# Scores and values of two attention heads issued by turns on two halves of the TensorE array

## The chip, the core and the metric

The kernel runs on one core of a Trainium2 chip. Its time is the device time of one execution in microseconds (us), taken as the median of three runs: 1239.64 us (1238.21 to 1241.14). The engines are TensorE (PE; its weight loads are shown as PEld), VectorE (DVE), ScalarE (ACT), GpSimd (POOL) and SyncE (SP, which here only issues transfers).

## The reference, cut to what matters

Two transformer blocks run one after the other on 256 tokens of width 1024. The first block has a pooling mixer beside an attention of 8 heads of 64 (att 1), then a feed-forward layer that picks 16 experts for each token and head. The second block has 8 heads with a forget gate and 8 heads with a banded mask and a relative bias (att 2, heads 0 to 7 and 8 to 15), then a convolutional feed-forward layer. Shortened, the attention parts are:

```python
# block 1, 256 positions are one block of keys: plain causal attention
s_own = jnp.einsum('bhcd,bhld->bhcl', q_c, k_own) * HEAD_DIM ** -0.5
p = jax.nn.softmax(jnp.where(k_pos <= q_pos, s_own, NEG), axis=-1)
o = jnp.einsum('bhcl,bhld->bhcd', p_own, v_own)

# block 2, heads 0 to 7: the logits also get a difference of running sums of log f
logits = jnp.einsum('bhqd,bhkd->bhqk', qb, k) * scale
logits = logits + cb[..., :, None] - cum[..., None, :]
# block 2, heads 8 to 15
logits = jnp.einsum('bhcqd,bhckd->bhcqk', qc, k_band) * (d ** -0.5) + bias
```

## The kernel before, in words

Every engine runs one program written out by hand, and waits on counters that the others raise. There is no planner for the stretches that change; the order in the code is the order on each queue. A name such as `("masked", att, i, tt)` is an event; `pe.wait_ge(made, ...)` waits for VectorE, `acted` for ScalarE, `done` for TensorE.

**Layout.** Queries and keys lie with two heads on the 128 partitions: the even head on partitions 0 to 63, the odd one on 64 to 127. A head's scores (`head_scores`, line 1460) are two fp32 products with 64 rows: 128 queries by 128 keys, and 128 queries by 256 keys, into one accumulator bank. Heads 0 to 7 of att 2 add to each a product with 8 rows that spreads the running sum of log f (`cum`). An fp32 product is two passes over the array, each with a load of its weights, so four records for a head of att 1 and eight for one with the forget gate. VectorE adds the mask and takes the row minimum (`masked`, line 925; the queries are scaled by -1/8, so it is the maximum of the logits), ScalarE takes exponentials (`exps`, 510), VectorE normalizes (`normed`, 909 and 912), TensorE transposes three 128x128 pieces (`turn`, 1468), ScalarE copies them out (`turned`, 517), and TensorE multiplies by the values (`values`, 1479 and 1480), with an output of 64 partitions: the even head's in the lower half of a bank, the odd head's in the upper half. VectorE or ScalarE reads that bank when both are there (`attended`, 938; `y_high`, 801; `attended_low`, 942).

**Order.** Both attentions are loops over steps i. On TensorE step i holds the scores of head i, then a large group of work that has nothing to do with this head (48 passes of projections with f32r weights, line 1408 or 1430, or branch products, 1559), then the transpose of head i-2, then the values of head i-3, then small products of the pooling mixer (1580, 1581, 1589). The same steps stand on VectorE: the mask of head i, `normed` of head i-1, splits of weights into a high and a low part (867), and in att 1 chunks of a matrix-vector product for the modulation (`ada`, 878). ScalarE has in step i the exponentials of head i, the copy of the step's projection (`copy_unit`, 504), roundings of weights (`split_high`, 500), and the transpose's copy. The steps of att 1 take 86 to 169 us of the profiled execution, those of att 2 922 to 1026 us.

**Banks.** There are eight accumulator banks. `Banks.take` gives the one freed first and lets TensorE wait for the event that frees it; `give` puts it back at the end of the queue, with that event, when the work is issued. So the order of all takes and gives decides which event each group of matmuls waits for:

```python
def take(self, pe, name):
    b, events = self.free.pop(0)
    self.where[name] = b
    for event in events:
        pe.wait_ge(*event)
```

A bank of scores is freed by the mask of its head, one of a projection by its copy, one of a transpose by `turned`.

Of the kernel before, what the change touches and what calls it, by code (L numbers as in the profile page):

```python
# [15 lines left out]
P = 128  # L16
T = 256
# [182 lines left out]
def build(nc, x_in, c_in, consts, bands_in, bmask_in, cols, relb, rows, w_ada, w_in, w_pool, w_br, w_out, w_q, keysT, uv, w_in2, w_f2,  # L200
          w_out2, w_up, w_down, out):
    with ExitStack() as ctx:
# [25 lines left out]
        probT = sb("probT", [P, 4, 384])  # L228
# [9 lines left out]
        ps = [ctx.enter_context(nc.psum_tensor(f"ps{i}", [P, 512], F32)) for i in range(8)]  # L238
# [12 lines left out]
        ident, ones = K("ident"), K("ones")  # L251
        ALL, tile = slice(0, T), [slice(0, P), slice(P, T)]
# [75 lines left out]
        cum, ncum = stat[0:8, 0:256], stat[0:8, 256:512]  # L328
# [13 lines left out]
        done = Mark(sem("s_pe"))  # L342
        acted = Mark(sem("s_act"))
        made = Mark(sem("s_dve"))
        marks = [*loaded, *half_loaded.values(), *once.values(), *arrived_in.values(), stored, high, low, done, acted, made]
        where = {}
# [41 lines left out]
        heads = {1: 8, 2: 16}  # L388
        cols_of = [slice(0, P), slice(P, 3 * P)]
# [993 lines left out]
        def tensor(e):  # L1383
            pe = Engine(e)
            banks = Banks(where)

            def group(name):
                return ps[banks.take(pe, name)]
# [59 lines left out]
                    ins.then_inc(*done.put(("rope", name, j0)))  # L1448
                    banks.give(("rope", name, j0), made, ("sin", name, j0))

            def head_scores(att, i):
                q3, k3, _, _, h = head_of(att, i)
                r, j = 64 * (h % 2), h // 2
                o = group(("heads", att, i))
                for tt in range(2):
                    terms = [(q3[r:r + 64, j, tile[tt]], k3[r:r + 64, j, 0:P + P * tt])]
                    if att == 2 and i < 8:
                        terms.append((ident[0:8, h:h + 1].broadcast_to([8, P]), cum[:, 0:P + P * tt]))
                    for m, (l, s) in enumerate(terms):
                        ins = e.matmul(o[:, cols_of[tt]], l, s, start=(m == 0), stop=(m == len(terms) - 1))  # L1460
                ins.then_inc(*done.put(("heads", att, i)))
                banks.give(("heads", att, i), made, ("masked", att, i, 1))

            def turn(att, i):
                o = group(("turn", att, i))
# [3 lines left out]
                ins.then_inc(*done.put(("turn", att, i)))  # L1469
                banks.give(("turn", att, i), acted, ("turned", att, i))  # L1470

            def values(att, i):
                _, _, v3, _, h = head_of(att, i)
                if i % 2 == 0:
                    group(("out", att, i // 2))
                r, pt = 64 * (i % 2), probT[:, i % 4, :]
                o = ps[where["out", att, i // 2]][r:r + 64, 0:T]
                pe.wait_ge(acted, ("turned", att, i))
                e.matmul(o, v3[:, 0, h * 64:(h + 1) * 64], pt[:, 0:T], start=True, stop=False)
                e.matmul(o[:, P:T], v3[:, 1, h * 64:(h + 1) * 64], pt[:, T:384], start=False, stop=True).then_inc(  # L1480
                    *done.put(("pv", att, i)))
                if i % 2:
                    banks.give(("out", att, i // 2), made, ("y", att, i // 2))

            def turned_rows(tt):

# [36 lines left out]
            for k0 in (0, 4):  # L1523
                pe.wait_ge(loaded[SLOT_OF["in", 0]] if k0 else half_loaded["in", 0], ("in", 0))
                for tt in range(2):
                    for k in range(k0, k0 + 4):
                        pe.wait_ge(acted, ("modulated", k))
                        ins = e.matmul(mixer[tt][:, :], h_sb[:, k, tile[tt]], w[:, k, :], start=(k == 0), stop=(k == KD - 1))
# [34 lines left out]
                    banks.give(("quarter", q), made, ("gated", 4 * br + z))  # L1563

            for i in range(11):
                if i < 8:
                    head_scores(1, i)
                if i < 7:
                    columns(*beside1[i], xs, lambda k: [], acted)
                if i >= 7:  # L1570
                    branch(0, i - 7)
                if 2 <= i <= 9:
                    turn(1, i - 2)
                if i >= 3:
                    values(1, i - 3)
                if i < 4:
                    o = group(("window", i))
                    pe.wait_ge(once["bands"], 0)
                    pe.wait_ge(acted, ("u", 1))
                    e.matmul(o[:, 0:T], ut[:, 0, i * P:(i + 1) * P], bands[:, i, 0:T], start=True, stop=False)  # L1580
                    e.matmul(o[:, P:T], ut[:, 1, i * P:(i + 1) * P], bands[:, i, T:T + P], start=False, stop=True).then_inc(
                        *done.put(("window", i)))
                    banks.give(("window", i), acted, ("window", i))
                if 1 <= i < 5:
                    g = i - 1
                    o = group(("mix", g))
                    pe.wait_ge(once["wp"], 0)
                    pe.wait_ge(acted, ("window", g))
                    e.matmul(o[:, 0:T], wp[:, g * P:(g + 1) * P], pT[:, g, :], start=True, stop=True).then_inc(
                        *done.put(("mix", g)))  # L1590
                    banks.give(("mix", g), acted, ("mix", g))

            for half in range(2):
                o = group(("gate1", half))
                pe.wait_ge(made, "mod2")
                for k in range(4):
                    c = 16 + 4 * half + k
                    ins = e.matmul(o[:, k * P:(k + 1) * P], mod[:, c:c + 1].broadcast_to([P, P]), ident, start=True,
                                   stop=True)
# [135 lines left out]
            for n in range(256):  # L1735
                tt, k = divmod(n, 128)
# [6 lines left out]
                for half in range(2):  # L1743
                    ins = e.matmul(acc[half][:, :], diag[:, n % 8, :],  # L1744
                                   row_buf[n][:, D + half * 512:D + (half + 1) * 512], start=(k == 0), stop=(k == 127))
# [27 lines left out]
            o = group("forget")  # L1773
            pe.wait_ge(made, "wf low")
            for k in range(KD):
                for n, (w, r) in enumerate(((wf_hi, hi_r), (wf_hi, lo_r), (wf_lo, hi_r))):
                    ins = e.matmul(o[0:8, 0:T], w[:, k, :], r[:, k, :], start=(k == 0 and n == 0),
                                   stop=(k == KD - 1 and n == 2))
# [31 lines left out]
            o = group("own sums")  # L1810
            pe.wait_ge(made, "ncum")
            for tt in range(2):
                ins = e.transpose(o[:, 8 * tt:8 * tt + 8], ncum[:, tile[tt]], ident[0:8, 0:8])
# [3 lines left out]
            for i in range(19):  # L1817
                if i == 8:
                    pe.wait_ge(acted, unit("in2", 4, 0))
                    pe.wait_ge(made, unit("in2", 4, 2))  # L1820
                    pe.wait_ge(acted, unit("in2", 3, 2))
                if i == 3:
                    pe.wait_ge(made, ("v", 2, 1))
                if i == 11:
                    pe.wait_ge(made, ("v", 5, 1))
                if i < 16:
                    head_scores(2, i)
                if i < 6:
                    kind, c, z = beside2[i]
                    if c == 5:  # L1830
                        tokens(kind, c, z, xs, both)
                    else:
                        columns(kind, c, z, xs, both, made if (c, z) == (4, 2) else acted)
                if 11 <= i < 15:
                    out2(0, (i - 11) // 2, (i - 11) % 2, range(4))
                if i == 17:
                    for half in range(2):
                        for tt in range(2):
                            out2(1, half, tt, range(2))
                if 2 <= i <= 17:  # L1840
                    turn(2, i - 2)
                if i >= 3:
                    values(2, i - 3)
            for tt in range(2):
                for half in range(2):
                    out2(1, half, tt, range(2, 4))
# [182 lines left out]
```

## Time and profile before

| | |
|---|---|
| median of three runs | 1239.64 us |
| the profiled execution | 1240.34 us, its span 1238.4 us |
| TensorE busy | 1092.4 us (88%) |
| VectorE busy | 821.9 us (66%) |
| ScalarE busy | 428.2 us (35%) |
| GpSimd busy | 292.4 us (24%) |
| mean granted TensorE clock | 0.955 of full speed |
| scores (line 1460), records | 96 with 64 rows, 32 with 8 rows |
| values (1479, 1480), records | 48 and 48 |

The span is the time from the first to the last instruction of the profiled execution. Matmuls are pipelined: a record's duration runs on into the next, so what a group costs is the distance of its start to the start of the next group. The expert rows are fetched between about 230 and 890 us.

### The profile page before, as it was taken

To read this page: it belongs to the slowest core of one execution; us is meant where nothing else is said; L and a number is where in the kernel's file an instruction comes from. 1 tells how busy PE (TensorE), PEld (TensorE's weight loads), DVE (VectorE), ACT (ScalarE), POOL (GpSimd) and SP (SyncE) were. 2 spreads that over 40 slices of the span, in tenths; PEclk is the share of its full clock that TensorE was granted. 3 is DMA by queue.
4 is the path that set the end of the run, shared out by engine and by line. 5 is a ranking of instruction groups with operands and counts; after the bars stand their busy time and mean duration, and the time that the engine had idled before them with its cause. 6 is when DMAs were issued, how large, how long until landed. Compare 5 with 4: busy or idle time off the path is not lost.

```text
span 1238.4 us, 13445 instructions
## 1 busy us (share of the span) xinstructions
PE 1092.4 (88%) x4938; PEld 723.5 (58%) x4938; DVE 821.9 (66%) x1891; ACT 428.2 (35%) x896; POOL 292.4 (24%) x260
## 2 busy tenths in 40 slices
PE   5999899899999987887788787788899999999997
PEld 3798785654445542333233333333698668999986
DVE  6696753767777677788877555545645545888753
ACT  3534441322322232122222111111554443666541
POOL 0000000345354442543544444443000000000000
PEclk8999899899999997988998999989999988999999
DMA  9977834799999999999999999999753311545530
GB/s 380 428 306 301 308 128 180 287 402 415 421 421 421 421 422 420 421 422 420 422 421 420 421 422 421 423 420 411 319 221 121 118 68 69 205 176 197 201 140 35
DMA packets 47878, 389.39 MB, mean 314 GB/s; under 512 B 5442, under 2 KB 5826, under 8 KB 7236
## 3 DMA queue, kind: packets, MB, share of 16 engines
q0 software_dynamic: 36864, 268.45, 52.3%
q1 hardware_dynamic: 10948, 120.07, 25.0%
q8 instruction: 40, 0.66, 0.2%
q14 instruction: 26, 0.21, 0.0%
HBM read 387.45 MB, written 1.05 MB: 314 GB/s over the span
## 4 chain that ended last, share of the span: by engine, by line
PE 52%; DMA 29%; DVE 12%; ACT 4%; issue 1%; POOL 1%; SPq 0%; DVEq 0%; POOLq 0%
DMA ring<-in_uv,idx 25%; PE ps L1408 16%; PE ps L1744 16%; PE ps L1869 5%; DMA ring<-in_w_ada 4%; DVE ring L1224 3%; PE ps L1614 2%; PE ps L1800 2%; PE ps L1559 2%; PE ps L1460 2%; PE ps L1430 2%; DVE ring_r L867 2%; DVE ring L878 2%; PE ps L1630 1%; POOL ring L484 1%
## 5 line engine op out<-in xcount | busy, mean ns | idle before, releaser
L1744 PE MATMUL ps<-ring,probT 128*128 128x512 f32 x1024 | 497.1, 631 | 106.9 <-ACT probT L732 106.8
L484 POOL DMA_INDIRECT ring<-in_uv,idx x256 | 292.2, 1141 | 563.5 <-PE ps L1744 307.0
L1224 DVE CUSTOM_DVE_ANT_0 ring<-h2t,ring 128x1024 f32<-128x1024 f32 x256 | 310.1, 1222 | 173.2 <-DMA ring<-in_uv,idx 172.8
L1744 PEld LDWEIGHTS ps<-ring,probT 128*128 128x128 f32 x1024 | 200.0, 201 | 354.0 <-issue 202.8
L1408 PE MATMUL ps<-util_r,ring_r 128*128 128x256 f32 x1312 | 216.6, 282 | 2.3 <-DVE ring_r L867 2.2
L867 DVE TENSOR_TENSOR ring_r<-ring,ring_r 128x1024 fp32r<-128x1024 f32 x134 | 158.3, 1220 | 54.7 <-ACT ring_r L500 54.7
L1408 PEld LDWEIGHTS ps<-util_r,ring_r 128*128 128x128 f32 x1312 | 181.0, 188 | 7.0 <-issue 3.9
L500 ACT ACTIVATE ring_r<-ring 128x1024 fp32r<-128x1024 f32 x134 | 134.6, 1049 | 46.5 <-DMA ring<-in_w_in 23.4
L727 ACT ACTIVATE prob<-prob 128x2 f32<-128x2 f32 (+2 forms) x94 | 19.2, 204 | 372.2 <-DVE prob L1224 372.1
L1408 PE MATMUL ps<-h_r,ring_r 128*128 128x256 f32 x704 | 125.2, 281 | 0.6 <-DVE util_r L1196 0.6
L732 ACT ACTIVATE probT<-ct,prob 128x128 f32<-128x128 f32 x256 | 85.1, 392 | 73.7 <-DVE prob L1230 73.5
L1408 PEld LDWEIGHTS ps<-h_r,ring_r 128*128 128x128 f32 x704 | 108.0, 188 | 0.8 <-issue 0.8
L878 DVE CUSTOM_DVE_ANT_0 ring<-h2t,ring 128x1024 f32<-128x1024 f32 x44 | 51.2, 1219 | 9.6 <-DMA ring<-in_w_ada 9.4
L1869 PE MATMUL ps<-ring_r,util_r 128*128 128x512 f32 x176 | 50.1, 395 | 0.0
L510 ACT ACTIVATE prob<-prob,mx 128x128 f32<-128x128 f32 (+1 forms) x48 | 21.5, 448 | 56.2 <-DVE mx L925 56.1
L1630 PEld LDWEIGHTS ps<-h_sb,ring 128*128 128x128 f32 x128 | 24.5, 192 | 24.8 <-issue 24.0
L1869 PEld LDWEIGHTS ps<-ring_r,util_r 128*128 128x128 f32 x176 | 32.9, 187 | 8.0
L1630 PE MATMUL ps<-h_sb,ring 128*128 128x256 f32 x128 | 36.0, 381 | 0.0
L1430 PE MATMUL ps<-ring_r,util_r 128*128 128x256 f32 x288 | 34.9, 281 | 0.0
L1430 PEld LDWEIGHTS ps<-ring_r,util_r 128*128 128x128 f32 x288 | 34.1, 188 | 0.7 <-issue 0.7
L1559 PE MATMUL ps<-area_r,ring_r 128*128 128x256 f32 x192 | 26.4, 301 | 6.1 <-DVE area_r L890 4.7
L1230 DVE TENSOR_TENSOR prob<-prob 128x2 f32<-128x2 f32 (+2 forms) x94 | 14.6, 155 | 23.2 <-ACT prob L727 23.2
(209 smaller groups left out, 1019.6 us busy)
## 6 DMA issues: line engine op xcount, KB each, us to landing
ring<-in_w_in SPq DMA_DIRECT2D x13, 2048.0 KB, 12.4
ring<-in_w_up SPq DMA_DIRECT2D x11, 2048.0 KB, 7.7
ring<-in_w_ada SPq DMA_DIRECT2D x7, 2048.0 KB, 7.7
ring<-in_w_down SPq DMA_DIRECT2D x6, 2048.0 KB, 7.7
ring<-in_w_ada SPq DMA_DIRECT2D x8, 1024.0 KB, 15.0
ring<-in_w_out SPq DMA_DIRECT2D x4, 2048.0 KB, 7.7
ring<-in_w_q SPq DMA_DIRECT2D x3, 2048.0 KB, 10.7
ring<-in_w_br SPq DMA_DIRECT2D x2, 2048.0 KB, 10.4
```

The lines of the kernel that those rows point to most:

```text
L484: e.indirect_dma_start(out=row_buf[n], out_offset=None, in_=uv, in_offset=bass.IndirectOffsetOnAxis(ap=idx[:, tt, k:k + 1], axis=0)).then_inc(
L500: e.activation(hi, w, ACT.Copy).then_inc(*high.put(q))
L732: e.activation(diag[:, n % 8, :], ident, ACT.Copy, scale=wt[:, tt, n % 128:n % 128 + 1]).then_inc(*acted.put(("diag", n)))
L867: e.tensor_tensor(lo, w, hi.bitcast(F32), ALU.subtract).then_inc(*low.put(q))
L878: e.tensor_tensor_reduce(wv, crow, wv, 1.0, 0.0, ALU.mult, ALU.add, mod[:, 4 * c + j:4 * c + j + 1]).then_inc(*made.put(("ada", c, j)))
L1224: e.tensor_tensor_reduce(u, h2t[:, tt, :], u, 1.0, 0.0, ALU.mult, ALU.add, av[:, tt, n % 128:n % 128 + 1]).then_inc(*made.put(("dot", n)))
L1408: ins = e.matmul(o[:, jj * T:(jj + 1) * T], w[:, k, :], r[:, k, :], start=(k == 0 and n == 0), stop=(k == KD - 1 and n == 2))
L1430: ins = e.matmul(o, r[:, k, tt * P:(tt + 1) * P], w[:, k, :, :], start=(k == 0 and n == 0), stop=(k == KD - 1 and n == 2))
L1559: ins = e.matmul(o[:, jj * T:(jj + 1) * T], w[:, k, jj * P:(jj + 1) * P], x3[:, k, :], start=(jj == 0 and k == 0 and n == 0), stop=(jj == ...
L1630: ins = e.matmul(bank(("q", h))[:, jj * T:(jj + 1) * T], w[:, k, z * P:(z + 1) * P], h_sb[:, k, :], start=(k == 0), stop=(k == KD - 1))
L1744: ins = e.matmul(acc[half][:, :], diag[:, n % 8, :], row_buf[n][:, D + half * 512:D + (half + 1) * 512], start=(k == 0), stop=(k == 127))
L1869: ins = e.matmul(ps[where["down", tt, half]][:, :], h[:, k, tile[tt]], w[:, 0, HALF[half]], start=(k == 0 and n == 0), stop=(k == KF - 1 a ...
```

## The change

`head_scores` becomes `pair_scores`. It is called in every even step and issues the scores of heads i and i+1: for each of the two query tiles first the even head's product on partitions 0 to 63, then the odd head's on 64 to 127, each into its own bank. With the forget gate the four products with 8 rows follow behind all four with 64 rows. Both banks are taken at the start of the step. `values` becomes `pair_values`, called in every even step from 4 on for heads i-4 and i-3, so that the even head's values come one step later than before, and the odd head's in the same step; the two write to the two halves of the output's partitions by turns. It waits for the later of the two transposed probabilities. In both loops the order of the rest stays. Two waits for the projected values move from steps 3 and 11 to 4 and 12.

```diff
-            def head_scores(att, i):
+            def pair_scores(att, i):
                 q3, k3, _, _, h = head_of(att, i)
-                r, j = 64 * (h % 2), h // 2
-                o = group(("heads", att, i))
+                j, summed = h // 2, att == 2 and i < 8
+                o = [group(("heads", att, i + a)) for a in range(2)]
                 for tt in range(2):
-                    terms = [(q3[r:r + 64, j, tile[tt]], k3[r:r + 64, j, 0:P + P * tt])]
-                    if att == 2 and i < 8:
-                        terms.append((ident[0:8, h:h + 1].broadcast_to([8, P]), cum[:, 0:P + P * tt]))
-                    for m, (l, s) in enumerate(terms):
-                        ins = e.matmul(o[:, cols_of[tt]], l, s, start=(m == 0), stop=(m == len(terms) - 1))
-                ins.then_inc(*done.put(("heads", att, i)))
-                banks.give(("heads", att, i), made, ("masked", att, i, 1))
+                    for a in range(2):
+                        r = slice(64 * a, 64 * a + 64)
+                        ins = e.matmul(o[a][:, cols_of[tt]], q3[r, j, tile[tt]], k3[r, j, 0:P + P * tt], start=(tt == 0),
+                                       stop=(tt == 1 and not summed))
+                        if tt == 1 and not summed:
+                            ins.then_inc(*done.put(("heads", att, i + a)))
+                if summed:
+                    for a in range(2):
+                        for tt in range(2):
+                            ins = e.matmul(o[a][:, cols_of[tt]], ident[0:8, h + a:h + a + 1].broadcast_to([8, P]),
+                                           cum[:, 0:P + P * tt], start=False, stop=(tt == 1))
+                        ins.then_inc(*done.put(("heads", att, i + a)))
+                for a in range(2):
+                    banks.give(("heads", att, i + a), made, ("masked", att, i + a, 1))
...
-            def values(att, i):
+            def pair_values(att, i):
                 _, _, v3, _, h = head_of(att, i)
-                if i % 2 == 0:
-                    group(("out", att, i // 2))
...
+                o = group(("out", att, i // 2))
+                pe.wait_ge(acted, ("turned", att, i + 1))
+                for s in range(2):
+                    for a in range(2):
+                        pt, v = probT[:, (i + a) % 4, :], v3[:, s, (h + a) * 64:(h + a + 1) * 64]
+                        ins = e.matmul(o[64 * a:64 * a + 64, P * s:T], v, pt[:, T * s:T * s + (P if s else T)],
+                                       start=(s == 0), stop=(s == 1))
+                        if s == 1:
+                            ins.then_inc(*done.put(("pv", att, i + a)))
+                banks.give(("out", att, i // 2), made, ("y", att, i // 2))
...
-                if i < 8:
-                    head_scores(1, i)
+                if i < 8 and i % 2 == 0:
+                    pair_scores(1, i)
...
-                if i >= 3:
-                    values(1, i - 3)
+                if i >= 4 and i % 2 == 0:
+                    pair_values(1, i - 4)
...
-                if i < 16:
-                    head_scores(2, i)
+                if i < 16 and i % 2 == 0:
+                    pair_scores(2, i)
...
-                if i >= 3:
-                    values(2, i - 3)
+                if i >= 4 and i % 2 == 0:
+                    pair_values(2, i - 4)
```

## Rows read from the trace of the kernel before

**Rows 1.** The chain of waits over the whole span, shares by engine

```profile
PE 52%; DMA 29%; DVE 12%; ACT 4%; issue 1%; POOL 1%; SPq 0%; DVEq 0%; POOLq 0%
```

**Rows 2.** Stage table: stretch, its length, busy us of each engine, granted clock, transfers

```profile
101.60:143.10 41.50, 41.50 (x307) 36.72 (x306) 28.80 (x74) 19.19 (x51) 0.00 (x0) 1.00 0.74 280
...
922.00:957.50 35.50, 35.50 (x246) 30.02 (x245) 17.74 (x36) 19.75 (x44) 0.00 (x0) 1.00 0.39 138
```

**Rows 3.** TensorE timeline, first attention: start, us, line, tiles, count, [idle before, releaser]

```profile
101.64 0.92 PE L1460 MATMUL ps<-area 64*128 64x128 f32 x4
102.48 5.95 PE L1408 MATMUL ps<-util_r,ring_r 128*128 128x256 f32 x48
...
109.78 0.92 PE L1460 MATMUL ps<-area 64*128 64x128 f32 x4
...
148.68 5.46 PE L1559 MATMUL ps<-area_r,ring_r 128*128 128x256 f32 x24 [4.67 <-DVE area_r L890]
...
155.23 3.12 PE L1559 MATMUL ps<-area_r,ring_r 128*128 128x256 f32 x24
...
165.09 3.10 PE L1559 MATMUL ps<-area_r,ring_r 128*128 128x256 f32 x24 [1.47 <-DVE util L933]
...
168.92 2.05 PE L1598 MATMUL ps<-ct,mod 128*128 128x128 f32 x16
```

**Rows 4.** VectorE timeline, first attention: masks of heads 1 and 5, copy of values

```profile
106.57 0.29 DVE L925 CUSTOM_DVE_ANT_0 prob<-ps,ct 128x128 f32<-128x128 f32 x1
...
134.86 0.28 DVE L925 CUSTOM_DVE_ANT_0 prob<-ps,ct 128x128 f32<-128x128 f32 x1
...
143.19 0.42 DVE L938 COPY area<-ps 128x256 f32<-128x256 f32 x1 [0.38 <-PE ps L1480]
```

**Rows 5.** ScalarE timeline, first attention: copy of step 4's projection

```profile
126.12 0.57 ACT L504 ACTIVATE util<-ps 128x512 f32<-128x512 f32 x1
```

**Rows 6.** TensorE timeline, second attention

```profile
922.15 0.48 PE L1460 MATMUL ps<-area 64*128 64x128 f32 x2
...
924.23 5.94 PE L1408 MATMUL ps<-util_r,ring_r 128*128 128x256 f32 x48
930.10 0.48 PE L1460 MATMUL ps<-area 64*128 64x128 f32 x2
...
954.60 0.65 PE L1479 MATMUL ps<-probT,area 128*64 128x256 f32 x2
...
955.40 0.48 PE L1460 MATMUL ps<-area 64*128 64x128 f32 x2
...
973.45 0.49 PE L1460 MATMUL ps<-area 64*128 64x128 f32 x2
...
1023.76 0.49 PE L1468 MATMUL ps<-ct,prob 128*128 128x128 f32 x3
```

**Rows 7.** The chain in order of time: start, us, engine, tile, line, count

```profile
250.27 0.86 PE ps L1630 x4
...
893.76 17.04 PE ps L1408 x144
```

**Rows 8.** Stage table around three idle stretches of TensorE, columns as in rows 2

```profile
148.70:153.90 5.20, 5.20 (x24) 5.20 (x25) 4.56 (x14) 0.99 (x4) 0.00 (x0) 0.50 0.91 315
...
842.40:846.10 3.70, 0.00 (x1) 0.01 (x1) 1.68 (x5) 0.66 (x3) 0.94 (x1) 1.00 1.01 421
847.00:850.30 3.30, 3.30 (x5) 1.35 (x4) 1.90 (x4) 0.00 (x0) 0.99 (x1) 0.50 1.03 427
...
987.00:997.00 10.00, 9.14 (x24) 5.75 (x23) 6.92 (x25) 6.81 (x18) 0.00 (x0) 0.50 0.01 2
```

**Rows 9.** VectorE timeline, second attention: masks of heads 2, 7 and 8

```profile
940.23 0.29 DVE L925 CUSTOM_DVE_ANT_0 prob<-ps,small 128x128 f32<-128x128 f32 x1 [2.80 <-PE ps L1460]
...
979.52 0.28 DVE L925 CUSTOM_DVE_ANT_0 prob<-ps,small 128x128 f32<-128x128 f32 x1
...
982.96 0.28 DVE L925 CUSTOM_DVE_ANT_0 prob<-ps,util 128x128 f32<-128x128 f32 x1
```

More of the change, by code:

```diff
@@ L1470, in turn @@
                 banks.give(("turn", att, i), acted, ("turned", att, i))
-            def values(att, i):
+            def pair_values(att, i):
                 _, _, v3, _, h = head_of(att, i)
-                if i % 2 == 0:
-                    group(("out", att, i // 2))
[L1476 to L1483, printed above, removed]
+                o = group(("out", att, i // 2))
[8 more added lines that the diff above has]
+                banks.give(("out", att, i // 2), made, ("y", att, i // 2))
             def turned_rows(tt):
@@ L1821, in tensor @@
                     pe.wait_ge(acted, unit("in2", 3, 2))
-                if i == 3:
+                if i == 4:
                     pe.wait_ge(made, ("v", 2, 1))
-                if i == 11:
+                if i == 12:
                     pe.wait_ge(made, ("v", 5, 1))
-                if i < 16:
-                    head_scores(2, i)
+                if i < 16 and i % 2 == 0:
+                    pair_scores(2, i)
                 if i < 6:
```

## The prediction, made before the changed kernel was run

> **What bounds the kernel now.** I read the chain of waits first: TensorE holds 52% of it, row fetches and weight loads 29%, VectorE 12% [rows 1]. The fetches are the expert-row loop between about 230 and 890 us, which the change does not touch. It touches two stretches, read in the stage table [rows 2]: the first attention (TensorE busy 41.5 of 41.5 us up to 143) and the second (35.5 of 35.5 us up to 957; behind 975 two other engines set the pace, [rows 9]). What is full there could gain from less TensorE work; but an engine that works without gaps in a fixed order also stops at the first wait that moves ahead of it. So the next views are the timelines of TensorE [rows 3, 6], VectorE [rows 4] and ScalarE [rows 5].
>
> **Price of a head now.** A 256-column fp32 pass takes 0.215 us (four in 0.86 us [rows 7]), a 128-column pass half, 0.11. A head's scores are two of each, 0.65 us, yet 0.84 us lie between their start and the next group's, 101.64 to 102.48 [rows 3]: 0.19 us more. The 48 passes between two heads' scores take 5.87 us, 924.23 to 930.10 [rows 6], against 5.68 for 48 in an undisturbed run (144 in 17.04 us [rows 7]): another 0.19 us. An entry and an exit thus cost 0.4 us together, 0.2 per change of form. It fits the forget-gate heads: 2.08 us (922.15 to 924.23 [rows 6]) for 1.30 us of passes, which is four changes (64 rows, 8 rows, 64, 8, 128). A head's values: 0.80 us (954.60 to 955.40 [rows 6]) for 0.65 us, so 0.15 for that change.
>
> **What the change removes.** Per pair of heads it removes an entry and an exit of the 64-row form and one entry of the half-column form: 0.55 us. With the forget gate, 12 changes become 4, so 8 go: 7 x 0.2 + 0.15 = 1.55 us. Four pairs of each of three kinds: 4 x 0.55 + 4 x 1.55 + 4 x 0.55 = 10.6 us of TensorE time. The passes themselves are as many as before.
>
> **Overlap of the two halves.** Nothing in the trace has two heads alternating, so I bound it. Full overlap makes a pair as long as one head: -0.65 us per pair of scores or values. The other end: each change of half costs like a change of form, three a pair, +0.6 us. Each pass needs its own weights first, and the second head follows the first only after both passes of its fp32 product, so most of a half's time cannot be shared: only the last pass of one and the first of the other could run together. I take -0.1 us per pair of scores and -0.2 per pair of values.
> The Trainium skill (TensorEngine Tiling (Array Packing), Key Properties) says that a change of tiling mode drains the array, which agrees with the 0.2 us above, and that tiles work independently of each other, for which no row here speaks. By that rule the overlap is nearer its full end, and the time is that of rival A.
>
> **The price in the first attention: banks.** Accumulator banks are handed out in a ring of eight, first freed first taken, and TensorE waits in program order. I wrote out the ring. Before, the group of 48 passes of step 2 (102.48) takes the bank of head 0. Now two heads take banks in step 0, so it takes that of head 1, which is free when VectorE has masked head 1. VectorE does that at 106.57 and ends about 107.2 [rows 4]; it comes after work on ada weights that TensorE does not influence. The ring written out this way names the gating product as what the last branch group waits for at 165.09, and the trace shows that wait, 1.47 us [rows 3].
> So TensorE, with step 2's pair done at about 103.1, stands until 107.3: 4.2 us. Its queue holds everything else of the stage. From there: 7.2 us to step 3's group (102.48 to 109.78 [rows 3], less the drain of the entry, 0.1), 114.5; its 5.8 us, transpose, window and mix, 1.6, to 121.9; pair (4,5), 1.5, 123.4; 48 passes end 129.2. ScalarE's copy of them was at 126.12 [rows 5], now 129.4, 3.3 later. Behind that copy in ScalarE's queue are two weight roundings, VectorE's two splits follow them, then its copy of values and an ada chunk, then the mask of head 5 at 134.86 [rows 4], now 138.2 to 138.8. Pair (6,7) takes the bank of head 5, so TensorE waits for that, 0.6 us. Then 1.5 + 5.8 + 0.4 + 1.5 us: the values of head 3 are ready at 148.1, where VectorE takes them at 143.19 [rows 4], with only 0.38 us of its own slack. Everything up to the branch group at 148.68 follows on that: **+4.9 us**.
> Given back behind it: from 148.68 to 168.92 [rows 3] are 20.24 us. Now: branch groups 5.26, 2.95, 2.95, 3.05; three transposes 1.26; two pairs of values 3.2; 18.7 in all. The 1.47 us wait is hidden, because the last branch group now takes another bank and the gated one falls to the values behind it: **-1.6 us**. What is late next there is nothing: the following matmuls run on without a gap to 200.
>
> **Clock.** Behind the 4.67 us stall before 148.68 the granted clock was 0.50 of full speed (the 1.2 GHz level) for 5.2 us, and 24 passes took 5.46 us where 24 take 3.12 at full clock [rows 3, 8]: 2.3 us. Behind 3.7 us of idleness up to 846.10 it was 0.50 too [rows 8]. The new stall of 4.2 us lies between those two, so I count a second such loss, **+2.3 us**; it passes through the same chain whole. Bounds: 0, and 5 us if it lasted as long as the 10 us from 987 to 997 [rows 8].
>
> **Second attention.** First five steps: three forget-gate pairs (0-1, 2-3, 4-5) and values 0-1, with heads 6 and 7 not begun. Before, 922.15 to 973.45 [rows 6] is 51.3 us. Now: 2.97 + 5.73 + 5.62 + 0.1, then 2.97 + 5.73 + 0.33 + 5.62 + 0.43, then 2.97 + 5.76 + 0.42 + 1.43 + 5.71 + 0.43 = 46.2 us: -5.1 us. No mask is late here: VectorE stands idle until TensorE's scores come (2.80 us before head 2 [rows 9]), so the banks are free in time. From 975 to 991 VectorE and ScalarE drive each other: mask, exponentials, rounding, split, next mask, 3.44 us a head (979.52 to 982.96 [rows 9]). The work of TensorE does not stand in that ring, so the 5 us stay and nothing is added. From 989 on TensorE is the bound again. Pairs (12,13) and (14,15) with their values take off 1.1. But VectorE masks head 15 only after its part of y from values 10 and 11, which come a step late, so the transposes of heads 13 to 15 wait for it: 1.6 to 2.3 us, and the values of head 12 fall behind that, 0.6: +2.9 in the upper case, which I take. The end (values 15, y, last products) keeps its distance to the last transpose at 1023.76 [rows 6]: values 14 now wait there too, 0.6 us, beside a rounding of ScalarE. Of the clock: from 987 to 997 it was 0.50 [rows 8], and TensorE lost some 3.2 us on the path from 989 on. At full clock the sum is -5.0 - 1.1 + 2.9 - 3.2 = **-6.4 us**. The stretch stays as loosely filled, so I expect the clock low again for 4 to 7 us of work on the path, half of which is lost: **+2.7**.
>
> **Sum.** +4.9 - 1.6 + 2.3 - 6.4 + 2.7 = +1.9 us. Overlap on the path (8 pairs of scores by 0.1, 7 of values by 0.2; others lie under stalls): -2.2. In all -0.3 us on the profiled execution's 1240.34 (span 1238.4 and 1.9 around it), which is 0.7 above the median 1239.64. A median is what will be compared, so I go from it: 1239.64 - 0.3 = 1239.34, told as **1239.3 us**: no change.
>
> **Rivals.**
> *A, the halves do overlap and the clock holds.* -0.2 per pair of scores and -0.4 of values make -4.4 instead of -2.2; without the low clock after 987, 2.7 less. 1.9 - 4.4 - 2.7 = -5.2: 1234.4 us; with the overlap alone -2.5, 1237.1. For it: separate rows, banks and columns. Against: the clock fell in that same loose stretch before [rows 8]. Chance 0.27.
> *B, slower: changing halves is a change of form.* If a pass on rows 64 to 127 drains what runs on rows 0 to 63, three changes a pair at 0.2 us return on each of the 8 score pairs on the path, +4.8, with no overlap: 1.9 + 4.8 = +6.7, 1246.3 us; if half of it is hidden, +4.3, 1243.9. Decisive from 0.1 us a change on. For it: the heads of [rows 6] pay 0.2 us for every change. Against: those are changes of size, and these are not. Together with a longer stall at 103 (a longer low clock, +0.8) chance 0.22.
> *C, no stall at 103.* If head 1's bank were not needed, only gains are left: -1.6 - 6.4 + 2.7 - 2.2 and 0.55 us from each of the two pairs before 143 = -8.6: 1231.0 us. Against it the wait at 165.09, which the ring names. Chance 0.06.
> The forecast keeps 0.45.
>
> **Range.** 1233.5 to 1244.5: A whole, the near half of B, not C. What this kernel's timings can tell from no change is about 0.2%, 2.5 us. Faster by more: A, C and a part of the forecast, 0.34. Slower: B and the forecast with no overlap and the longer low clock, 0.25. Within: 0.41.
>
> **What would show it.** In the timeline of TensorE after: a stall of about 4 us after the second pair of scores, ended by VectorE's mask (wrong, if TensorE goes on at 103); a granted clock of 0.50 behind it; the stall at 165.09 gone; the branch group of 148.68 near 153 to 156; the first pair of scores of the second attention at about 3.0 us where two heads took 4.2; the last transpose minus the first score 95 instead of 101.6 us. A pair of scores without the forget gate shows the overlap: 1.5 us from its start to the next group's is none, 1.3 and less is overlap, 2.1 is rival B. The forecast is wrong if the two stretches do not move in opposite directions by about 5 us each.

## The result and the profile after

The changed kernel takes 1231.84 us, the median of five runs (1230.42 to 1232.97); the kernel before, beside it, 1239.48. The ratio is 0.993, with a 95% interval of 0.9917 to 0.9943: 7.6 us faster, where no change was forecast and the range ended at 1233.5. The profiled execution took 1231.68 us, its span is 1229.8 (before 1238.4). TensorE was busy for 1080.7 us (88%), VectorE 821.5, ScalarE 428.9, GpSimd 289.9, and the mean granted clock was 0.937 of full speed (0.942 to 0.950 in the other four runs), lower than the 0.955 of before.

The shares of the chain of waits are those of [rows 1] within a point, so this view does not tell where the time went:

```profile
PE 52%; DMA 29%; DVE 13%; ACT 3%; issue 1%; POOL 1%; SPq 0%; DVEq 0%; POOLq 0%
```

The timeline of TensorE in the first attention answers to [rows 3] (start, us, engine, line, tiles, count, [idle before, releaser]; 1459 are now the scores, 1488 the values, 1476 the transposes, 1568 the branches, 1607 the groups that were 1598):

```profile
101.63 0.93 PE L1459 MATMUL ps<-area 64*128 64x128 f32 x8
107.26 8.58 PE L1408 MATMUL ps<-util_r,ring_r 128*128 128x256 f32 x48 [4.70 <-DVE mx L925]
...
124.28 0.93 PE L1459 MATMUL ps<-area 64*128 64x128 f32 x8
125.14 5.95 PE L1408 MATMUL ps<-util_r,ring_r 128*128 128x256 f32 x48
...
131.35 0.87 PE L1488 MATMUL ps<-probT,area 128*64 128x256 f32 x8
132.15 0.70 PE L1598 MATMUL ps<-area,h2t 128*128 128x256 f32 x2
...
140.58 0.93 PE L1459 MATMUL ps<-area 64*128 64x128 f32 x8 [1.73 <-DVE mx L925]
...
154.06 4.64 PE L1568 MATMUL ps<-area_r,ring_r 128*128 128x256 f32 x24 [5.56 <-DVE area_r L890]
...
166.11 3.08 PE L1568 MATMUL ps<-area_r,ring_r 128*128 128x256 f32 x24
169.12 0.87 PE L1488 MATMUL ps<-probT,area 128*64 128x256 f32 x8
169.92 2.05 PE L1607 MATMUL ps<-ct,mod 128*128 128x128 f32 x16
```

Three things are to be seen. The stall after the second pair of scores is there, ended by VectorE's mask as the ring of banks had it, and a second one before the last pair. The wait of 1.47 us before the last branch group is gone. And a group of eight score records takes 0.86 us to the next group's start (124.28 to 125.14), the same as four did in [rows 3] (0.84 us); eight of the values take 0.80 us (131.35 to 132.15), as four did in [rows 6]. A pair costs as much as one head.

The second attention, same view, answers to [rows 6]:

```profile
924.60 0.93 PE L1459 MATMUL ps<-area 64*128 64x128 f32 x8
925.46 1.57 PE L1466 MATMUL ps<-stat,ct 8*128 8x128 f32 x8
926.96 11.62 PE L1408 MATMUL ps<-util_r,ring_r 128*128 128x256 f32 x96
...
975.56 0.55 PE L1476 MATMUL ps<-ct,prob 128*128 128x128 f32 x3 [1.66 <-DVE prob L912]
976.89 1.55 PE L1488 MATMUL ps<-probT,area 128*64 128x256 f32 x8 [0.78 <-ACT probT L517]
979.82 1.65 PE L1459 MATMUL ps<-area 64*128 64x128 f32 x8
...
1006.68 0.52 PE L1476 MATMUL ps<-ct,prob 128*128 128x128 f32 x3 [1.80 <-DVE prob L912]
...
1017.38 0.49 PE L1476 MATMUL ps<-ct,prob 128*128 128x128 f32 x3
```

The first two heads with the forget gate end after 2.36 us (924.60 to 926.96), where one took 2.08. From the first score to the last transpose are 92.8 us; it was 101.6.

The stage table of after (stretch, length, busy us of TensorE, its weight loads, VectorE, ScalarE and GpSimd, granted clock, transfers) shows first the two stretches of [rows 2], then those in which the clock was low, and one that was low before:

```profile
101.60:143.10 41.50, 35.07 (x265) 32.73 (x265) 25.25 (x65) 16.53 (x44) 0.00 (x0) 0.88 0.65 242
922.00:957.50 35.50, 35.50 (x287) 32.87 (x286) 20.21 (x46) 21.57 (x49) 0.00 (x0) 1.00 0.43 154
...
107.30:113.20 5.90, 5.90 (x28) 5.90 (x29) 1.73 (x9) 2.56 (x10) 0.00 (x0) 0.50 0.96 347
150.80:157.60 6.80, 3.54 (x17) 3.57 (x17) 6.80 (x15) 0.16 (x1) 0.00 (x0) 0.50 0.90 340
976.80:990.30 13.50, 11.15 (x41) 7.26 (x42) 9.97 (x34) 8.87 (x26) 0.00 (x0) 0.50 0.09 37
1007.60:1014.20 6.60, 6.19 (x19) 4.65 (x20) 4.47 (x7) 2.92 (x5) 0.00 (x0) 0.50 0.37 156
1020.00:1036.00 16.00, 13.16 (x86) 11.22 (x85) 9.36 (x23) 6.17 (x12) 0.00 (x0) 1.00 0.36 132
```

Of the kernel before, the same view at the same place of the program as the last row:

```profile
1034.80:1041.40 6.60, 6.54 (x30) 6.02 (x28) 1.11 (x1) 1.72 (x3) 0.00 (x0) 0.50 0.63 271
```

The time by stages, before and after, from starts in the two timelines:

| start of | before | after | difference, and step |
|---|---|---|---|
| first branch group | 148.68 | 154.06 | +5.4 |
| line 1598 / 1607 | 168.92 | 169.92 | +1.0, so -4.4 |
| first score, second attention | 922.15 | 924.60 | +2.5, so +1.5 |
| its last transpose | 1023.76 | 1017.38 | -6.4, so -8.8 |
| first product behind the second attention (1408) | 1044.95 | 1036.31 | -8.6, so -2.3 |
| end of the span | 1238.4 | 1229.8 | -8.6, so 0 |

### The profile page after: what moved, and what is told of

It reads as the page before. It is cut to its first block, busy times and chain, and to the rows that moved or that the text cites. A ratio compares the mean times of both kernels' runs of the same rounds, so it can differ in the third digit from the quotient of the medians.

```text
span 1229.8 us, 13453 instructions
## 1 busy us (share of the span) xinstructions
PE 1080.7 (88%) x4938; PEld 717.4 (58%) x4938; DVE 821.5 (67%) x1891; ACT 428.9 (35%) x896; POOL 289.9 (24%) x260
## 4 chain that ended last, share of the span: by engine, by line
PE 52%; DMA 29%; DVE 13%; ACT 3%; issue 1%; POOL 1%; SPq 0%; DVEq 0%; POOLq 0%
DMA ring<-in_uv,idx 25%; PE ps L1753 16%; PE ps L1408 16%; PE ps L1878 5%; DMA ring<-in_w_ada 4%; DVE ring L1224 3%; DVE ring L878 2%; PE ps L1623 2%; PE ps L1809 2%; DVE ring_r L867 2%; PE ps L1568 2%; PE ps L1430 2%; PE ps L1639 2%; POOL ring L484 1%; ACT L727 1%
## 5 line engine op out<-in xcount | busy, mean ns | idle before, releaser
L1753 PE MATMUL ps<-ring,probT 128*128 128x512 f32 x1024 | 507.8, 643 | 97.5 <-ACT probT L732 97.4
L1753 PEld LDWEIGHTS ps<-ring,probT 128*128 128x128 f32 x1024 | 204.3, 205 | 349.6 <-issue 208.6
L1408 PE MATMUL ps<-util_r,ring_r 128*128 128x256 f32 x1312 | 219.6, 285 | 6.4 <-DVE mx L925 4.7
L1408 PEld LDWEIGHTS ps<-util_r,ring_r 128*128 128x128 f32 x1312 | 184.2, 192 | 9.7 <-DVE mx L925 5.4
```

Of the source, the lines that this page charges most:

```text
L1408: ins = e.matmul(o[:, jj * T:(jj + 1) * T], w[:, k, :], r[:, k, :], start=(k == 0 and n == 0), stop=(k == KD - 1 and n == 2))
L1753: ins = e.matmul(acc[half][:, :], diag[:, n % 8, :], row_buf[n][:, D + half * 512:D + (half + 1) * 512], start=(k == 0), stop=(k == 127))
```

## The experiments

All are timed against the kernel before, which gave 1239.66, 1240.59 and 1239.99 us in the three sets of runs. Line numbers move a little from kernel to kernel.

**By turns, or only next to each other?**

```diff
 # pair_scores; pair_values likewise with s
-                for tt in range(2):
-                    for a in range(2):
+                for a in range(2):
+                    for tt in range(2):
```

> The changed kernel, but within each pair the first head's products are all issued before the second head's, for scores and for values; steps, banks and waits are the same. Theory 1 (the halves of the array run at the same time only because products on the two halves stand next to each other in the queue, and this overlap of 0.64 us a pair is what the prediction sized too small): a pair goes back from 0.86 to about 1.5 us, with some 8 pairs of scores and 7 of values on the path +9 us, 1239 to 1241 us. Theory 2 (each half has its own queue of products, so it looks ahead over a whole head of four passes): a pair stays at 0.86 us and the time at 1232. Rival (the gain comes from fewer changes of form and from the clock, and the overlap lies under stalls): a pair at 1.5 us, but the time within 2 us of 1232.

Measured: 1231.91 us (1230.91 to 1232.08), ratio 0.9938 (0.9921 to 0.9954), the time of the changed kernel, as theory 2 has it. Three narrow windows of TensorE's timeline, each from just before the first score record, tell how close the records start. The changed kernel, up to 101.80:

```profile
101.63 0.38 PE L1459 MATMUL ps<-area 64*128 64x128 f32 x2
```

This kernel, up to 102.02:

```profile
101.99 0.39 PE L1459 MATMUL ps<-area 64*128 64x128 f32 x2
```

The kernel before, up to 101.80:

```profile
101.64 0.37 PE L1460 MATMUL ps<-area 64*128 64x128 f32 x1
```

Two records of 0.37 us each lie in 0.38 and 0.39 us: both halves start at once, although in this kernel all passes of the first head stand ahead of the second head's in the queue. That the second record is the other head's shows in the forms. Of this kernel's line 1459, the records from 101.98 to 102.25:

```profile
L1459 PE MATMUL ps<-area x4: 272/322/373, 102.0 to 102.2; 64*128 64x128 f32 x4
```

These are all four passes with 128 keys, two of each head, and none yet with 256 keys, though the first head's two of these stand ahead of the second head's in the queue. The turns of the change add nothing; heads on different halves that stand next to each other are enough. The Trainium skill (TensorE: Matmul & The Clock Gate, Part 3: Packing small matmuls) says that matmuls start and end strictly in the order of the program; here a second head's first pass starts beside the first head's first pass and thus before its second, so the trace does not bear that out, while the page's picture of packed tiles starting almost together fits.

**Is it the halves?** The odd head's queries and keys are taken from the partitions of the even one, so both heads use rows 0 to 63; the kernel leaves out the odd heads' scores. Everything else stays.

```diff
-                        r = slice(64 * a, 64 * a + 64)
+                        r = slice(0, 64)
```

> The changed kernel, but both heads of a pair take their scores from partitions 0 to 63, so the odd heads use the even head's queries and keys; instruction counts, banks, waits and changes of form are the same. Theory 1 (different row halves are what lets two products run at the same time, worth 0.64 us a pair): a pair of scores takes 1.50 us instead of 0.86, with 6 to 8 of 12 pairs on the path +4 to +5 us, 1236 to 1237 us. Rival (two products into different banks overlap in any case, or the pairs are hidden): 1232 us.

Measured: 1239.17 us (1236.64 to 1242.47), ratio 0.9994 (0.9982 to 1.0006). TensorE's timeline:

```profile
101.68 1.57 PE L1459 MATMUL ps<-area 64*128 64x128 f32 x8
107.31 0.58 PE L1408 MATMUL ps<-util_r,ring_r 128*128 128x256 f32 x1 [4.06 <-DVE mx L925]
...
927.16 1.57 PE L1459 MATMUL ps<-area 64*128 64x128 f32 x8
928.66 1.57 PE L1466 MATMUL ps<-stat,ct 8*128 8x128 f32 x8
930.16 13.14 PE L1408 MATMUL ps<-util_r,ring_r 128*128 128x256 f32 x96
```

The pair takes 1.50 us (927.16 to 928.66) instead of 0.86: 0.64 more, which is the whole of the second head. The first theory has the cause right, and its time is 2 us too low. Without the overlap of the scores the kernel is no faster than before, although it has all the savings in changes of form, and its values still overlap (0.80 us a pair). That its time is near the one I had forecast (1239.3) is chance. Of the 7.3 us between this kernel and the changed one, the overlap of the 8 pairs of scores that I had counted on the path explains 5.1. The rest goes with a cost that I had not expected: behind the first pair of the second attention 96 passes take 13.14 us for 11.62, and the 48 behind the third pair and behind the last pair of the first attention take 1.5 us more each, at the low clock. The run does not separate the two.

**What must stand next to what?** In the pairs with the forget gate each head's 8-row products go right behind its own 64-row ones: 64, 8, 64, 8 instead of 64, 64, 8, 8.

```diff
                 if summed:
                     for a in range(2):
+                        r = slice(64 * a, 64 * a + 64)
+                        for tt in range(2):
+                            e.matmul(o[a][:, cols_of[tt]], q3[r, j, tile[tt]], k3[r, j, 0:P + P * tt], start=(tt == 0), stop=False)
                         for tt in range(2):
                             ...
```

> The changed kernel, but in the pairs with the forget gate each head's two products with 8 rows stand right behind its own two with 64 rows, so that the two heads' 64-row products are no longer neighbours in the queue. Theory (what overlaps is only what stands next to each other and uses other rows): the pair goes from 2.36 us to 2.36 + 0.65 (overlap lost) + 0.4 (two more changes of form) = 3.4 us or more; three to four such pairs on the path make +3 to +4 us: about 1235.5 us. Rival (a head on the upper rows runs beside whatever is ahead of it, the 8-row products too): only the two changes are paid, 2.8 us a pair, +1.5 us: 1233.3 us.

Measured: 1239.71 us (1235.07 to 1241.25), ratio 0.9991 (0.998 to 1.0002). Line 1467 holds the products with 64 rows here, 1469 those with 8:

```profile
941.53 0.92 PE L1467 MATMUL ps<-area 64*128 64x128 f32 x4
942.38 0.92 PE L1469 MATMUL ps<-stat,ct 8*128 8x128 f32 x4
943.23 0.92 PE L1467 MATMUL ps<-area 64*128 64x128 f32 x4
944.07 0.92 PE L1469 MATMUL ps<-stat,ct 8*128 8x128 f32 x4
944.92 7.47 PE L1408 MATMUL ps<-util_r,ring_r 128*128 128x256 f32 x48
```

The pair takes 3.39 us (941.53 to 944.92) for 2.36, so 1.03 more, which is the overlap of 0.64 and two changes of form at 0.2: the first theory. Nothing on the upper rows runs beside the 8-row products ahead of it. But the total is 4 us above what that theory gave. Four such pairs cost 4.1; from first score to last transpose are 101.8 us (925.08 to 1026.92) for 92.8, so 4.9 us are left, and most of them stand behind the pairs, as the stage table shows for the second:

```profile
945.00:950.00 5.00, 5.00 (x30) 5.00 (x31) 4.96 (x11) 2.03 (x3) 0.00 (x0) 0.66 0.65 279
```

The clock, at 1.00 throughout this stretch of the changed kernel, is at 0.66 behind the pair of 3.4 us, and 48 passes take 7.3 us for 5.8. The same holds behind the first pair (96 passes, 12.9 us for 11.6) and the third (48, 7.3 for 5.7): 4.4 us in all. I had not expected that. That nothing else takes part was not tested.

**Scores alone, values alone.** `pair_scores` or `pair_values` is put back to the form of before, with its call:

```diff
 # scores only; the loop of the second attention likewise
-                if i >= 4 and i % 2 == 0:
-                    pair_values(1, i - 4)
+                if i >= 3:
+                    values(1, i - 3)
 # values only
-                if i < 8 and i % 2 == 0:
-                    pair_scores(1, i)
+                if i < 8:
+                    head_scores(1, i)
```

> Only the scores are paired; values head by head in their old steps. Theory 1: the stall at 103 us stays (two score banks are taken in one step), the second attention gains about 1.8 us for each of the four forget-gate pairs and 1 us for each later pair on the path: 1236 us. Rival (scores and values gain alike, or values more): 1238 or more.

> Only the values are paired; scores head by head in their old steps. Theory 1: no stall at 103 us, since the order in which banks are freed does not move until step 3; each pair of values on the path (two behind 148 us, four or five in the second attention) takes off 0.8 us, which makes 5 us: 1234.5 us. Rival (values lie under waits for ScalarE's copy): 1238 or more.

Measured: scores alone 1237.37 us (1236.07 to 1238.53), ratio 0.9978 (0.9968 to 0.9987); values alone 1234.13 (1231.99 to 1237.13), 0.9949 (0.9933 to 0.9966). The timelines of the first attention, scores alone (1567 are the branches):

```profile
107.47 7.84 PE L1408 MATMUL ps<-util_r,ring_r 128*128 128x256 f32 x48 [4.70 <-DVE mx L925]
...
154.49 5.33 PE L1567 MATMUL ps<-area_r,ring_r 128*128 128x256 f32 x24 [5.52 <-DVE area_r L890]
...
170.73 1.45 PE L1567 MATMUL ps<-area_r,ring_r 128*128 128x256 f32 x10 [1.47 <-DVE util L933]
```

and values alone (1560 are the branches, 1599 the groups that were 1598):

```profile
148.84 5.07 PE L1560 MATMUL ps<-area_r,ring_r 128*128 128x256 f32 x24 [6.01 <-DVE area_r L890]
...
161.33 3.08 PE L1560 MATMUL ps<-area_r,ring_r 128*128 128x256 f32 x24
165.14 2.05 PE L1599 MATMUL ps<-ct,mod 128*128 128x128 f32 x16
```

The stall at 103 belongs to the scores, and the end of the 1.47 us wait to the values (by the ring, to the later taking of their bank). Values alone bring line 1599 3.8 us forward (168.92 to 165.14); scores alone bring the second attention, first score to last transpose, from 101.6 to 91.9 us, values alone only to 99.6. The two parts gain in different attentions. Finer differences there tell nothing: the code of the changed kernel's second attention takes 90.4 to 92.8 us in the four profiles that have it.

**One attention at a time.** The unchanged attention keeps `head_scores` and `values`:

```diff
 # second only; first only has the same in the loop of the second
-                if i < 8 and i % 2 == 0:
-                    pair_scores(1, i)
+                if i < 8:
+                    head_scores(1, i)
```

> The second attention paired, the first as before. Theory 1 (the second attention gives 9 us, the first loses 1 and the row loop does not differ): 1239.7 - 9 to 11, 1229 to 1231 us, a little faster than the changed kernel. Rival (a part of the 9 us is the clock after 1034 us, which falls or not by chance): 1233.

> The first attention paired, the second as before. Theory 1: the two stalls and the second low clock cost 5.4 us up to the branch group, 4.4 come back behind it: 1239.7 + 1, between 1240 and 1242 us. Rival (the first attention gains on balance): 1238 or less.

Measured: second alone 1230.54 us (1227.92 to 1231.22), ratio 0.9916 (0.9897 to 0.9936); first alone 1240.81 (1237.84 to 1244.15), 1.0003 (0.999 to 1.0015). In the first attention all that the pairs save is eaten by the stall; the gain of the change is the second attention's.

**Does the bank make the stall?** In the first attention the odd head's bank goes back to the queue one step later, so that the next taker is given another; first for heads 1, 3, 5 and 7, then for 1, 3 and 5:

```diff
-                for a in range(2):
+                for a in range(2 if att == 2 or i == 6 else 1):
                     banks.give(("heads", att, i + a), made, ("masked", att, i + a, 1))
 # at the end of step i of the first attention
+                if i < 6 and i % 2:
+                    banks.give(("heads", 1, i), made, ("masked", 1, i, 1))
```

> The changed kernel, with one edit: in the first attention the bank of each odd head goes back into the ring at the end of the next step, so no group of that step takes it. Theory 1 (the stall of 4.7 us at 103 us, the one of 1.7 us at 139 us and the low clock behind the first one cost what the first stretch lost): both stalls gone, the branch group at 148.5 us instead of 154.1, the 1.5 us wait before the last branch group is back: 5 us less, 1227 us. Rival (VectorE's chain of splits, ada chunks and copies ends that stretch anyway and TensorE's delay was mostly hidden): less than 2 us, 1230 or more.

> The kernel with the late banks of the first attention, but only for heads 1, 3 and 5; head 7's bank goes back at once, as in the changed kernel. Written out, the ring then gives the last branch group the bank of an output (free early) and the waiting values the one of the gating product. Theory 1 (what the late banks won before 148 us was lost again in that wait and in the low clock behind it, 2.3 + 1.6 us): branch group at 148 us and no wait at 163, the following products start at about 165 us instead of 169; 1.5 to 4 us less than the 1229 us with all banks late: 1226 us. Rival (the wait for the gating product only moves to the values): 1229.

Measured: four heads 1229.01 us (1226.53 to 1230.83), ratio 0.991 (0.989 to 0.9931); three heads **1225.44** us (1224.54 to 1226.22), 0.9882 (0.9866 to 0.9899), which beats both kernels. Four heads stay 2 us above what the theory gave. With them the stalls at 103 and 139 go, but the ring moves a wait to the last branch group:

```profile
148.23 5.46 PE L1568 MATMUL ps<-area_r,ring_r 128*128 128x256 f32 x24 [7.27 <-DVE area_r L890]
...
163.76 4.62 PE L1568 MATMUL ps<-area_r,ring_r 128*128 128x256 f32 x24 [2.26 <-DVE util L933]
169.12 2.05 PE L1609 MATMUL ps<-ct,mod 128*128 128x128 f32 x16
```

With three it is gone as well:

```profile
101.72 0.93 PE L1459 MATMUL ps<-area 64*128 64x128 f32 x8
102.58 5.94 PE L1408 MATMUL ps<-util_r,ring_r 128*128 128x256 f32 x48
...
148.19 5.46 PE L1568 MATMUL ps<-area_r,ring_r 128*128 128x256 f32 x24 [8.79 <-DVE area_r L890]
...
165.28 2.05 PE L1609 MATMUL ps<-ct,mod 128*128 128x128 f32 x16
```

The branch group starts at 148.19, 0.5 us ahead of before, though TensorE now stands idle for 8.79 us before it: VectorE's product (line 890) sets that start, and up to there the saving of TensorE is worth nothing. Behind it the stage is shorter.

**Do the values of the second attention need pairing?** The version above, with `values` of before in the second attention:

```diff
-                if i >= 4 and i % 2 == 0:
-                    pair_values(2, i - 4)
+                if i >= 3:
+                    values(2, i - 3)
```

> The version with the later bank for heads 1, 3 and 5 (1225.4 us), but in the second attention the values run head by head as in the kernel before; scores stay paired. Theory: in the second attention it is the paired scores that bring the gain (scores alone left 92.1 us from first score to last transpose, values alone 99.8), because the odd head's earlier transposes and y then come a step sooner again; so about 1225 us, within 1.5 of the version it is derived from. Rival: paired values count by their overlap (0.6 us each) and by the change of form they save; five pairs lie on TensorE's path, so 3 to 4 us are lost: 1228.5 us.

Measured: 1226.67 us (1225.27 to 1226.97), ratio 0.9891 (0.9877 to 0.9905) beside 0.9882 (0.9866 to 0.9899). The intervals overlap; pairing these values is worth some 1 us, as the theory had it, against 3 to 4 us by the rival. That is a net: head by head, the even head's values also come a step sooner, and the run does not tell what the overlap brings from what the delay costs.

## Why the prediction was wrong, step by step

The step that failed is the size of one term: "I take -0.1 us per pair of scores and -0.2 per pair of values." It measured -0.64 per pair of scores (0.86 us where two heads one behind the other take 1.50), and for a pair of values as much: 0.80 us is the 0.65 of one head's passes and one change of form at 0.15. That is the full end of my bounds. My reason for the small end was that the second head follows the first only after both passes of its fp32 product; the head-by-head kernel shows that its passes do not wait for them, nor for the rest of the first head. With 15 pairs on the path, as I had counted, the term is -9.6 us instead of -2.2, and the sum 1.9 - 9.6 = -7.7: 1231.9 us, against 1231.84 measured. With the overlap of the scores taken out, that of the values left in, the kernel took 1239.17.

The size of the overlap per pair is shown. That the sum then fits this closely is luck: how many pairs lie on the path was never measured, and against the two profiles, 8.6 us apart where the medians are 7.6, other terms were off by 0.1 to 2.3 us, both ways:

- *Price of a change of form, 0.2 us.* Held: 2.36 us for the pair with the gate is 0.65 + 1.30 of passes and two changes, and 3.39 us for the order 64, 8, 64, 8 is 1.30 + 1.30 and four.
- *Stall in the first attention.* Held: 4.70 us of idleness for 4.2, the wait for the mask of head 5 1.73 for 0.6, the branch group 5.4 us late where 4.9 and 2.3 for the clock, less the overlap of three pairs (1.9), make 5.3. Both waits for a mask were read from the ring of banks written out by hand, and the later bank removed them.
- *-1.6 behind the branch group.* It was -4.4. Two pairs of values overlap (-1.3); the first branch group took 4.48 us to the next start (154.06 to 158.54) for 5.26 (-0.8); the 3.2 us for the values still held the change of form that a pair saves (-0.3); and two of the three transposes took 0.24 us for 0.42 (-0.4), for instance 165.87 to 166.11, because no values follow them now. The hidden wait of 1.47 held.
- *Second low clock, +2.3.* It came, from 107 to 113: 48 passes took 8.42 us, 107.26 to 115.68, that take 5.8, so 2.6. Behind the same stall the head-by-head kernel lost only 1.4.
- *Second attention, -6.4 + 2.7 = -3.7.* With the ten pairs that are left of the fifteen overlapped (-6.4) that is -10.1; measured -8.8, and by the spread above the same code can give -11.2.
- *Behind it*, where I expected nothing, -2.3 us: the low clock of before (0.50 for 6.6 us in the row above) did not come. There was more of it earlier, 20.1 us of low clock in the second attention (976.80 to 990.30 and 1007.60 to 1014.20) for about 10 in [rows 8].
- *Between 170 and 922 us*, where I had counted nothing, +1.5 us. The code there is the same in all twelve kernels, and from the modulation (1598 or 1607) to the first score their profiles take 752.8 (three late banks) to 757.3 us (scores alone): 1.5 us lies within that spread, and is no effect that these runs can show.

Of the rivals, A had the right sign and a cause of which half is true: the overlap, but at 0.2 and 0.4 us a pair, and a clock that holds, which it did not inside the attention. B, a change of half as a change of form, is refuted: a pair would have taken 2.1 us. C, no stall at 103, was wrong of this kernel, and its time (1231.0) was near for another reason. With the stall really taken away the kernel stands at 1225.4. The signs I had named for right and wrong worked: "1.3 and less is overlap" points straight at the term.

The Trainium skill (TensorEngine Tiling (Array Packing), Key Properties) says that tiles execute weight loads and matmuls in parallel. The trace now agrees, with 0.86 us for two heads; the forecast had set it aside because no row of before showed two heads next to each other. Where the trace says nothing for or against a stated rule, the rule deserves more than the chance of 0.27 that I gave rival A.

## What to carry to other kernels

Fp32 products that use half the rows (or half the output partitions) came in at half price here when the two halves stood next to each other in the queue, by turns or not, with no product of another form between them; look first for a pair that an 8-row product or a projection keeps apart. Count the saving only where TensorE is the bound, and write out the ring of accumulator banks before two are taken at once: here that stall ate all of the first attention's gain, and giving a bank back one step later returned 6 us. Price the clock by what stands ahead of a full group of work, since a stretch that gets looser can lose at half clock what it saved.

## What the runs showed of the hardware

- Two fp32 products on rows 0 to 63 and 64 to 127 overlap completely: 0.86 us for the pair, 0.84 for one, 1.50 for two on the same rows. Values into the two halves of the output partitions do too: 0.80 us for a pair, 0.80 for one.
- A second head's first pass starts within 0.02 us of the first head's first, ahead of the first head's second.
- A pass on rows 64 to 127 does not run beside an 8-row product ahead of it: 0.85 us from one group's start to the next, as for a head alone.
- The granted clock fell to its lower level (0.50, 1.2 GHz) not only behind idleness. In the first 45 us of the second attention TensorE has no gap. The seven profiles with gate pairs of 2.36 us show no fall there; with pairs of 3.00 us it fell behind two of three, with pairs of 3.39 us behind all three. Of three profiles with single heads of 2.08 us one shows a fall, in values alone, so the length of the narrow stretch is not all that decides:

```profile
924.26 7.47 PE L1408 MATMUL ps<-util_r,ring_r 128*128 128x256 f32 x48
```

- The same code can meet either clock. Up to the second pair of scores the kernels with four and with three late banks have the same code in the first attention, and behind that pair the one took 7.32 us for its 48 passes (102.60 to 109.92), the other 5.78 (102.58 to 108.36):

```profile
102.60 7.48 PE L1408 MATMUL ps<-util_r,ring_r 128*128 128x256 f32 x48
```
